# Moving the selection of keys, the products after a scan, and a load within a hybrid decoder layer's kernel

## The chip, the cores and the metric

The kernel runs on one core of a Trainium2 chip. Its time is the device time of one execution in microseconds (us), shown as the median of several runs. The engines are TensorE (PE in the profile; its weight loads are PEld), VectorE (DVE), ScalarE (ACT), GpSimd (POOL) and SyncE (SP), which here only issues transfers. Each engine works through its own queue in order, and engines wait for one another by semaphores.

## The reference, cut to what matters

One layer of a decoder runs for a prompt of 1040 rows (16 learned rows and 1024) and for 64 sample rows. All rows are normed and projected by one wide matrix `w_in`. Branch A keeps for each query the 256 best admissible keys by an index score and attends over them. Branch B is stick-breaking attention:

```python
z = q @ k.T * HEAD_DIM ** -0.5
log_keep = where(strict, log_sigmoid(-z), 0)
after = reverse_cumsum(log_keep) - log_keep
out = exp(where(strict, log_sigmoid(z) + after, -inf)) @ v
```

The kernel computes branch B without logarithms: the weight of a key is sigmoid(z) times the product of sigmoid(-z) over all later keys up to the query. The product is a scan from right to left, and the weights are one elementwise product after it. Gates, a gated convolutional MLP and a last norm follow; the change does not touch them.

## The kernel before, in words

The program is a row of blocks, each with a barrier at its end: norm, index projections, index scores of samples and prompt, the other projections, stick (branch B), sparse (branch A), sample attention, merge, MLP, last norm. Three of its parts are touched.

**Projections** (`projections`, tag `pr`). Five pairs of column blocks, 512 columns each; the last pair is followed by none. For each half s of pair k PE multiplies nine row tiles (`NT`) by a weight block that is split in a high and a low part (ScalarE L324, VectorE L352, from the raw weights in `w_raw`), and the result goes by a ring of six tiles to the array `proj` in memory (SP L310). VectorE has time over there: it runs a bisection (`Bisection`) for the 256th largest score of every row, over the seven tiles with more than 256 keys (`INDEX_TILES`, widths 384 to 1024 and 1040, 5264 columns together). One bit takes a count per tile (L827) and some small steps; seven bits go into each of five pairs, 35 passes for 31 bits. `part` deals them out over the 18 half-tiles of a pair. The split of the next weights stands behind the fourth tile of a half (`SPLIT_AT`), so VectorE waits there for ScalarE and for nothing else of the matmuls in the last three pairs.

**Selection** turns the threshold into additive masks in bf16 (0 or -1e30): `next_threshold`, seven counts above it, and five steps per tile (`choose`: equality L944, a scan that ranks equals L946, a comparison L948, an addition L950, a scaling L952), 42 parts in all. VectorE takes two parts at the end of each of the first 21 iterations of stick.

**Stick** (`stick`). Four pairs of heads (`PAIRS`), nine query tiles each, so 36 iterations n, with lags written out by hand. Rows of q and k are loaded at the block's start and for each next pair (L1043, L1044), turned by PE (L1091) and copied by ScalarE. For tile t the keys are (t + 1) * 128 columns, 1040 in the last tile, which has only 16 rows. Iteration n:

```python
score(n); turn_qk(...)       # PE L1103, L1109, L1091
turn(n - 3); use(n - 4)      # PE L1122, then L1137
open_tile(n); take_qk(...)   # ScalarE L1178, L1179
take_turns(n - 3)            # ScalarE L1189
scan both heads of n         # VectorE L1219
evacuate(n - 5)              # VectorE L1211
product for both heads of n  # GpSimd L1077
```

`score` makes the scores of a tile in four banks of PSUM, up to 512 columns each; `open_tile` takes two sigmoids from each bank (`rest`, `prob`); VectorE scans `rest`; GpSimd multiplies `prob` by it; `turn` transposes the weights, four tiles to a bank and two banks in turn, which `take_turns` copies; `use` multiplies them by the values into one of two tiles `o`, and waits until the tile two before has been evacuated. Four buffers of `prob` and `rest` let the engines be some tiles apart. The text calls `turn` the turns, `use` the value products and the tile t the tile's number within its pair.

The store of the sample rows' mask stands near the end of SP's queue. The masks have a tensor of their own, which sparse reads.

Of the kernel before, what the change touches and what calls it, by code (L numbers as in the profile page):

```python
# [40 lines left out]
P = 128  # L41
D = 1024
KC = D // P
# [28 lines left out]
NEG = -1e30  # L72
LEAST = -3e38
# [163 lines left out]
def projections(nc, ctx, tag, w_in, cos, sin, hi, lo, w_raw, raw_in, done, proj, head, plain_pairs, behind, search):  # L237
# [52 lines left out]
    with nc.Block() as block:  # L290
        @block.sync
        def _(sp):
# [51 lines left out]
        def _(dve):  # L344
            dve.wait_ge(tables_in, 32)
            turns = Count(turned_by)

# [36 lines left out]
            def body(k, two, following):  # L384
                for s in range(2):
                    for t in range(NT):
# [4 lines left out]
                        if search:  # L391
                            search.part(dve, k, NT * s + t, 2 * NT)
# [274 lines left out]
MASK_AT, MASKS_W = packed(range(NT))  # L667
# [126 lines left out]
class Bisection:  # L794
# [5 lines left out]
    PER = -(-BITS // TURNS)  # L800
# [21 lines left out]
    def count_tile(self, dve, j, op, flags=None):  # L822

        if flags is None:
            t = INDEX_TILES[j]
            flags = self.flags[:, SCORE_AT[t]:SCORE_AT[t] + key_width(t)]
        return dve.tensor_scalar(flags, self.of_tile(j), self.thr[:, j:j + 1], None, op, ALU.add,  # L827
                                 accum_out=self.count[:, j:j + 1])
# [18 lines left out]
    def part(self, dve, i, n, parts):  # L847

        steps, tiles = self.steps, len(INDEX_TILES)
        for x in range(n * self.PER * tiles // parts, (n + 1) * self.PER * tiles // parts):  # L850
# [23 lines left out]
class Selection:  # L874
# [4 lines left out]
    STEPS = 6  # L879
    PER = 5  # L880
    ALL_MADE = 4 + PER * len(INDEX_TILES)

    def __init__(self, nc, ctx, search, masks):
        def sb(name, shape, dt=F32):
            return ctx.enter_context(nc.sbuf_tensor(f"tk_{name}", shape, dt))
        self.search, self.masks = search, masks
        self.equal = [sb(f"equal{b}", [P, NP_ROWS]) for b in range(2)]
        self.rank = [sb(f"rank{b}", [P, NP_ROWS]) for b in range(2)]
        self.low_half, self.high_half, self.carry = (sb(n, [P, len(INDEX_TILES)], I32)
                                                     for n in ("low_half", "high_half", "carry"))  # L890
# [16 lines left out]
    def next_threshold(self, dve):  # L907
# [3 lines left out]
        halves = self.halves  # L911
        dve.tensor_scalar(low_half, mag, 0xFFFF, None, ALU.bitwise_and)
# [14 lines left out]
    def count_above(self, dve, j):  # L927
# [26 lines left out]
    def part(self, dve, n):  # L954

        tiles = len(INDEX_TILES)
        if n == 0:
            self.next_threshold(dve)
# [1669 lines left out]
```

## Time and profile before

| what | value |
|---|---|
| runs shown | 2531.18, 2535.61, 2536.31 us; median 2535.61 |
| profiled execution, its own time | 2532.94 us |
| its span, first to last instruction | 2531.3 us |
| PE, DVE, ACT, POOL busy | 2197.9, 1479.0, 772.8, 182.8 us |
| mean granted clock of PE | 0.941 |

The span is shorter than the execution's time by what lies around it. A busy time is the union of an engine's instructions; PE's matmuls overlap, and their ends are modelled. Shares of the whole span are averages over stages with different limits. The page's chain that ended last holds only the last norm, about 6 us, so the stages have to be read one by one.

### The profile page before, as it was taken

How to read it: one execution, taken by the hardware profiler on the slowest of the kernel's cores; microseconds unless marked ns; L12 is line 12 of the kernel's file. 1: busy time of each engine (PE TensorE's matmuls, PEld its weight loads, DVE VectorE, ACT ScalarE, POOL GpSimd, SP SyncE). 2: the span in 40 equal slices, each digit the busy share in tenths (PEclk: the TensorE clock that was granted, in tenths of full speed). 3: DMA queues.
4: the chain of work that ended last, by engine and by line, in shares of the span. 5: the costliest groups of instructions: out<-in, count | busy, mean ns of one | idle time of the engine just before them, and what ended most of it. 6: DMA issues, size and time to landing. Idle time of an engine off the chain costs nothing. (4 is left out here: it accounts for less than half of the span.)

```text
span 2531.3 us, 37719 instructions
## 1 busy us (share of the span) xinstructions
PE 2197.9 (87%) x13473; PEld 1812.3 (72%) x13473; DVE 1479.0 (58%) x2563; ACT 772.8 (31%) x1449; POOL 182.8 (7%) x141
## 2 busy tenths in 40 slices
PE   3867799999997777788488698979999999999995
PEld 3823488888885555555355487869999999999994
DVE  4416878567574997457144355335655665665566
ACT  4025310121113656567133333122212212221212
POOL 0001000000002677000100000000000000000000
PEclk8978899999998988899699899989999999999998
DMA  3212122222312110220699844011011101111102
GB/s 130 78 37 53 57 84 91 105 83 81 114 50 73 37 37 12 56 73 18 185 367 362 322 147 178 2 46 51 25 50 50 46 29 50 50 33 42 50 17 87
DMA packets 186022, 218.75 MB, mean 86 GB/s; under 512 B 28796, under 2 KB 119292, under 8 KB 184764
## 3 DMA queue, kind: packets, MB, share of 16 engines
q1 hardware_dynamic: 177588, 214.02, 25.7%
q10 hardware_dynamic: 8072, 3.05, 0.5%
q8 instruction: 66, 1.08, 0.2%
q0 software_dynamic: 256, 0.27, 0.1%
q14 instruction: 40, 0.33, 0.0%
HBM read 181.17 MB, written 36.13 MB: 86 GB/s over the span
## 5 line engine op out<-in xcount | busy, mean ns | idle before, releaser
L2385 DVE TENSOR_TENSOR x_all<-x_all,ff_down 128x512 f32<-128x512 f32 x396 | 272.3, 688 | 163.6 <-PE ff_down L2289 158.9
L2274 PE MATMUL ff_up<-m_hi,ff_up_hi 128*128 128x368 f32 x1056 | 348.6, 330 | 7.5 <-DVE ff_up_lo L2362 7.5
L2275 PE MATMUL ff_up<-m_lo,ff_up_hi 128*128 128x368 f32 x1056 | 348.9, 330 | 0.0
L2276 PE MATMUL ff_up<-m_hi,ff_up_lo 128*128 128x368 f32 x1056 | 348.4, 330 | 0.0
L411 PE MATMUL pr_acc<-pr_w_hi,h_hi 128*128 128x512 f32 x720 | 281.5, 391 | 16.2 <-DVE pr_w_lo L352 16.2
L412 PE MATMUL pr_acc<-pr_w_lo,h_hi 128*128 128x512 f32 x720 | 281.3, 391 | 0.0
L413 PE MATMUL pr_acc<-pr_w_hi,h_lo 128*128 128x512 f32 x720 | 281.0, 390 | 0.0
L827 DVE TENSOR_SCALAR_CACHE_REDUCE bi_flags<-scores,bi_thr 128x384 bf16<-128x384 f32 (+6 forms) x252 | 235.4, 993 | 1.3
L2274 PEld LDWEIGHTS ff_up<-m_hi,ff_up_hi 128*128 128x128 f32 x1056 | 199.0, 188 | 8.8 <-DVE ff_up_lo L2362 7.9
L2275 PEld LDWEIGHTS ff_up<-m_lo,ff_up_hi 128*128 128x128 f32 x1056 | 199.0, 188 | 0.9
L2276 PEld LDWEIGHTS ff_up<-m_hi,ff_up_lo 128*128 128x128 f32 x1056 | 198.9, 188 | 0.0
L411 PEld LDWEIGHTS pr_acc<-pr_w_hi,h_hi 128*128 128x128 f32 x720 | 135.8, 189 | 44.8 <-DVE pr_w_lo L352 16.3
L336 ACT ACTIVATE pr_staged<-pr_acc 128x512 f32<-128x512 f32 x72 | 43.1, 599 | 399.8 <-PE pr_acc L413 399.8
L2287 PE MATMUL ff_down<-ff_down_hi,ff_g_hi 128*128 128x512 f32 x396 | 157.5, 398 | 5.8 <-issue 5.8
L1077 POOL TENSOR_TENSOR st_prob<-st_prob,st_rest 128x127 f32<-128x127 f32 (+8 forms) x72 | 155.6, 2184 | 82.4 <-DVE st_rest L1219 82.4
L1219 DVE TENSOR_TENSOR_SCAN st_rest<-st_rest 128x128 f32<-128x128 f32 (+8 forms) x72 | 121.7, 1728 | 65.1 <-ACT st_prob L1179 65.0
L2289 PE MATMUL ff_down<-ff_down_hi,ff_g_lo 128*128 128x512 f32 x396 | 157.1, 397 | 0.0
L2288 PE MATMUL ff_down<-ff_down_lo,ff_g_hi 128*128 128x512 f32 x396 | 157.0, 397 | 0.0
L413 PEld LDWEIGHTS pr_acc<-pr_w_hi,h_lo 128*128 128x128 f32 x720 | 135.9, 189 | 28.3
L412 PEld LDWEIGHTS pr_acc<-pr_w_lo,h_hi 128*128 128x128 f32 x720 | 135.9, 189 | 28.2
L2316 ACT ACTIVATE ff_g_hi<-ff_g 128x1152 fp32r<-128x1152 f32 x22 | 25.7, 1168 | 299.9 <-DVE ff_g L2370 299.9
L352 DVE TENSOR_TENSOR pr_w_lo<-w_raw,pr_w_hi 128x2048 fp32r<-128x2048 f32 x20 | 44.9, 2288 | 118.1 <-ACT pr_w_hi L324 118.1
(283 smaller groups left out, 3728.3 us busy)
## 6 DMA issues: line engine op xcount, KB each, us to landing
out_proj<-pr_staged SPq DMA_DIRECT2D x90, 256.0 KB, 2.0
up_raw<-in_w_up SPq DMA_DIRECT2D x44, 512.0 KB, 5.0
w_raw<-in_w_in SPq DMA_DIRECT2D x10, 2048.0 KB, 7.9
sa_keys<-in_cache_k_a SPq DMA_DIRECT2D x64, 256.0 KB, 4.3
sa_keys<-in_cache_k_b SPq DMA_DIRECT2D x64, 256.0 KB, 7.3
sa_values<-in_cache_v_a SPq DMA_DIRECT2D x64, 256.0 KB, 7.8
sa_values<-in_cache_v_b SPq DMA_DIRECT2D x64, 256.0 KB, 5.4
ff_down_raw<-in_w_down SPq DMA_DIRECT2D x22, 512.0 KB, 3.6
```

The source lines that it names most:

```text
L411: pe.matmul(out, hi[:, c, at], w_hi[s][:, c, 0:width], start=c == 0, stop=False)
L412: pe.matmul(out, hi[:, c, at], w_lo[s][:, c, 0:width], start=False, stop=False)
L413: ins = pe.matmul(out, lo[:, c, at], w_hi[s][:, c, 0:width], start=False, stop=c == KC - 1)
L827: return dve.tensor_scalar(flags, self.of_tile(j), self.thr[:, j:j + 1], None, op, ALU.add, accum_out=self.count[:, j:j + 1])
L1077: pool.tensor_tensor(x, x, rest[g % R][hh][0:r, 1:w], ALU.mult).then_inc(weighed, 1)
L2274: pe.matmul(up[n][:], w, hi[:, c, at], start=c == 0, stop=False)
L2275: pe.matmul(up[n][:], w, lo[:, c, at], start=False, stop=False)
L2276: ins = pe.matmul(up[n][:], w_rest, hi[:, c, at], start=False, stop=c == KC - 1)
L2287: pe.matmul(down[n][:], g_hi[:, at], down_hi[:, cols], start=True, stop=False)
L2288: pe.matmul(down[n][:], g_hi[:, at], down_lo[:, cols], start=False, stop=False)
L2289: pe.matmul(down[n][:], g_lo[:, at], down_hi[:, cols], start=False, stop=True).then_inc(down_done, 1)
L2385: dve.tensor_tensor(at, at, down[n][:], ALU.add).then_inc(down_added.sem, 1)
```

## The change

1. The bisection has 28 bits in the first four pairs and its last 3 in the first half of the last pair. The selection runs in the second half of that pair, on VectorE, 42 parts over nine tiles. Its steps are recast: a [P,1] step, an equality that gives 2^100 or 0 in bf16, a scan, a comparison with a product, and one step that makes the mask.
2. The masks lie over the scores of their own tile; the two full tiles' masks lie behind them. The selection's scratch tiles lie in `w_raw`, behind the rows below. `w_raw` lives until sparse has ended.
3. The first pair's rows of q and k for stick are loaded into `w_raw` during the last half block of the projections, after the last weight split and after all stores of the pairs before.
4. In stick, the products after the scan move from GpSimd to VectorE, behind both scans of the tile. The value products of tile n - 4 stand ahead of the turns of tile n - 3. Results of tiles 0 to 3, 4 to 7 and 8 of a head pair share a bank, and are evacuated by one copy each. The store of the sample mask moves to the head of SP's queue.

The diff, cut to its core (signatures and renamed arguments are left out):

```diff
@@ projections, SyncE @@
                     if coming:
                         sp.wait_ge(lo_made, 2 * k + s + 1)
                         load(coming)
+                    elif load_ahead:
+                        sp.wait_ge(lo_made, 2 * k + s + 1)
+                        for b in range(RING):
+                            sp.wait_ge(stored[b], 16 * 3 * k)
+                        load_ahead(sp)
...
@@ projections, VectorE @@
-                        if search:
-                            search.part(dve, k, NT * s + t, 2 * NT)
+                        if selection and following:
+                            search.part(dve, k, NT * s + t, 2 * NT, search.PER)
+                        elif selection and s == 0:
+                            search.part(dve, k, t, NT, search.LAST)
+                        elif selection:
+                            selection.part(dve, t, NT)
...
-MASK_AT, MASKS_W = packed(range(NT))
+MASK_AT = {t: 2 * SCORE_AT[t] for t in INDEX_TILES}
+MASK_AT.update({t: 2 * SCORE_AT[NT - 1] + key_width(NT - 1) + at for t, at in packed(range(FULL_T))[0].items()})
...
@@ Bisection @@
-    PER = -(-BITS // TURNS)
+    PER = 7
+    LAST = BITS - PER * (TURNS - 1)
...
@@ Selection @@
-    ALL_MADE = 4 + PER * len(INDEX_TILES)
+    PARTS = len(INDEX_TILES) * (1 + PER)
+    ALL_MADE = 3 + PER * len(INDEX_TILES)
...
+        self.search = search
+        self.masks = search.scores[:].bitcast(BF16)
+        self.rank = spare[:, 0:NP_ROWS]
+        self.equal = spare[:, NP_ROWS:NP_ROWS + NP_ROWS // 2].bitcast(BF16)
...
-    def count_above(self, dve, j):
-
-        ins = self.search.count_tile(dve, j, ALU.is_gt, self.of_tile(INDEX_TILES[j]))
+    def count_not_above(self, dve, j):
+
+        ins = self.search.count_tile(dve, j, ALU.is_le)
...
         if step == 0:
-            dve.tensor_scalar(eq, self.search.of_tile(j), self.search.thr[:, j:j + 1], None, ALU.is_equal).then_inc(ended, 1)
+            dve.tensor_scalar(need, search.count[:, j:j + 1], BIG, BIG * (TOPK - w), ALU.mult, ALU.add).then_inc(ended, 1)
         elif step == 1:
+            dve.tensor_scalar(eq, search.of_tile(j), search.thr[:, j:j + 1], BIG, ALU.is_equal, ALU.mult).then_inc(ended, 1)
+        elif step == 2:
             dve.tensor_tensor_scan(rk, eq, eq, 0.0, ALU.add, ALU.bypass).then_inc(ended, 1)
-        elif step == 2:
-            dve.scalar_tensor_tensor(rk, rk, self.search.need[:, j:j + 1], eq, ALU.is_le, ALU.mult).then_inc(ended, 1)
         elif step == 3:
-            dve.tensor_tensor(eq, rk, self.of_tile(t), ALU.add).then_inc(ended, 1)
+            dve.scalar_tensor_tensor(rk, rk, need, eq, ALU.is_le, ALU.mult).then_inc(ended, 1)
         else:
-            dve.tensor_scalar(self.of_tile(t), eq, -1.0, -NEG, ALU.add, ALU.mult).then_inc(ended, 1)
...
+            dve.scalar_tensor_tensor(self.of_tile(t), search.flags_of(j), -BIG, rk, ALU.mult, ALU.add).then_inc(ended, 1)
...
+        for x in range(n * self.PARTS // parts, (n + 1) * self.PARTS // parts):
+            if x == 0:
+                self.next_threshold(dve)
+            if x < tiles:
+                self.count_not_above(dve, x)
+            else:
+                self.choose(dve, *divmod(x - tiles, self.PER))
...
@@ stick @@
+    O_GROUPS = [(0, 4), (4, 8), (8, NT)]
+    group_of = [next(k for k, (a, b) in enumerate(O_GROUPS) if a <= t < b) for t in range(NT)]
...
-    o = [ctx.enter_context(nc.psum_tensor(f"st_o{b}", [P, P], F32)) for b in range(2)]
+    o = [ctx.enter_context(nc.psum_tensor(f"st_o{b}", [P, 4 * P], F32)) for b in range(2)]
...
@@ stick, SyncE @@
-            load_qk(0)
+            selection.store(sp, sample_mask, mask_stored)
...
-            selection.store(sp, sample_mask, mask_stored)
-            sp.wait_ge(o_out, NG)
+            sp.wait_ge(mask_stored, 16)
+            sp.wait_ge(o_out, PAIRS * len(O_GROUPS))
...
@@ stick, GpSimd @@
             selection.allow_all(pool)
-            for g in range(NG):
-                r, w = tile_rows(g % NT), key_width(g % NT)
-                for hh in range(2):
-                    pool.wait_ge(scanned, 2 * g + hh + 1)
-                    x = prob[g % R][hh][0:r, 0:w - 1]
-                    pool.tensor_tensor(x, x, rest[g % R][hh][0:r, 1:w], ALU.mult).then_inc(weighed, 1)
...
@@ stick, TensorE: use(g) @@
-                if g >= 2:
-                    pe.wait_ge(o_out, g - 1)
+                b = i * len(O_GROUPS) + group_of[t]
+                first, last = O_GROUPS[group_of[t]]
+                at = (t - first) * P
+                if t == first and b >= 2:
+                    pe.wait_ge(o_out, b - 1)
...
-                        ins = pe.matmul(o[g % 2][half(hh), 0:r], v_rows[i % 2][0:w, kt, half(hh)],
-                                        prob_t[g % 2][hh][0:w, kt, 0:r], start=kt == 0, stop=kt == t)
+                        ins = pe.matmul(o[b % 2][half(hh), at:at + r], v_rows[i % 2][0:w, kt, half(hh)],
+                                        prob_t[g % 2][hh][0:w, kt, 0:r], start=kt == 0, stop=kt == t,
+                                        skip_group_check=True)
...
+                if n >= USE_LAG:
+                    use(n - USE_LAG)
                 if TURN_LAG <= n < NG + TURN_LAG:
                     turn(n - TURN_LAG)
-                if n >= USE_LAG:
-                    use(n - USE_LAG)
...
@@ stick, VectorE @@
+            def evacuate(i, k):
+                first, last = O_GROUPS[k]
+                b = i * len(O_GROUPS) + k
+                dve.wait_ge(used, i * NT + last)
+                if k == 0 and i >= 2:
+                    dve.wait_ge(stored[i % 2], 16 * (i // 2))
...
+                w = min(last * P, NP_ROWS) - first * P
+                dve.tensor_copy(o_all[i % 2][:, first * P:first * P + w], o[b % 2][:, 0:w]).then_inc(o_out, 1)
...
+                for hh in range(2) if n < NG else ():
+                    dve.wait_ge(scanned, 2 * n + hh + 1)
+                    x = prob[n % R][hh][0:r, 0:w - 1]
+                    dve.tensor_tensor(x, x, rest[n % R][hh][0:r, 1:w], ALU.mult).then_inc(weighed, 1)
                 if n >= USE_LAG + 1:
-                    evacuate(n - USE_LAG - 1)
-                selection.part(dve, 2 * n)
-                selection.part(dve, 2 * n + 1)
+                    i, t = divmod(n - USE_LAG - 1, NT)
+                    if t + 1 == O_GROUPS[group_of[t]][1]:
+                        evacuate(i, group_of[t])
...
@@ program @@
+                w_raw = index_scope.enter_context(nc.sbuf_tensor("w_raw", [P, KC, 512], F32))
+                behind_weights = w_raw[:].rearrange("p c n -> p (c n)")
+                q_rows, k_rows = (behind_weights[:, ROWS * k:ROWS * (k + 1)].rearrange("p (t n) -> p t n", t=NT)
+                                  for k in range(2))
+                selection = Selection(nc, index_scope, search, behind_weights[:, 2 * ROWS:])
...
+                def load_stick(sp):
+                    sp.dma_start(q_rows, tiled[:, :, O_QB:O_QB + P]).then_inc(stick_in, 16)
+                    sp.dma_start(k_rows, tiled[:, :, O_KB:O_KB + P]).then_inc(stick_in, 16)
```

## Rows read from the trace of the kernel before

**Rows 1.** Busy time by stretch, two stages: us, then PE, PEld, DVE, ACT, POOL; clock, DMA
```profile
268.00:780.00 512.00, 493.51 (x2168) 407.70 (x2164) 347.14 (x782) 81.90 (x99) 1.66 (x7) 0.98 0.24 84
780.00:1032.00 252.00, 191.67 (x1536) 135.97 (x1536) 198.00 (x166) 147.45 (x385) 157.02 (x78) 0.86 0.14 38
```

**Rows 2.** The same view, the stick stage by head pair
```profile
791.70:838.20 46.50, 35.08 (x216) 21.63 (x216) 44.00 (x51) 32.49 (x83) 27.61 (x16) 0.84 0.21 53
838.20:901.50 63.30, 48.26 (x386) 35.08 (x385) 58.96 (x46) 36.52 (x96) 39.54 (x19) 0.87 0.17 45
901.50:959.60 58.10, 45.58 (x387) 32.07 (x386) 53.21 (x38) 36.27 (x96) 44.13 (x18) 0.91 0.07 20
959.60:1030.00 70.40, 58.65 (x536) 43.48 (x534) 41.82 (x34) 39.40 (x104) 44.29 (x21) 0.85 0.03 11
```

**Rows 3.** Timeline of PE, six score products, one group of value products: start us, us, operation
```profile
808.52 2.01 PE L1103 MATMUL st_banks<-st_k_t,st_q_t 64*128 64x512 f32 x8
...
923.99 2.08 PE L1103 MATMUL st_banks<-st_k_t,st_q_t 64*128 64x512 f32 x4
...
928.12 1.35 PE L1103 MATMUL st_banks<-st_k_t,st_q_t 64*128 64x512 f32 x8
...
935.53 1.77 PE L1103 MATMUL st_banks<-st_k_t,st_q_t 64*128 64x512 f32 x8
...
959.59 0.72 PE L1103 MATMUL st_banks<-st_k_t,st_q_t 64*128 64x128 f32 x4
...
963.16 1.53 PE L1137 MATMUL st_o<-st_prob_t,st_v_rows 128*64 128x128 f32 x24
...
978.63 2.08 PE L1103 MATMUL st_banks<-st_k_t,st_q_t 64*128 64x512 f32 x4
```

**Rows 4.** Who waited for whom, 923.99 to 978.63: us in total, times, longest
```profile
PE st_turned L1122 <- ACT st_prob_t L1189: 3.6, 4, 1.2
...
PE st_turned L1122 <- POOL st_prob L1077: 2.3, 1, 2.3
...
PE st_o L1137 <- DVE st_o_all L1211: 0.6, 1, 0.6
```

**Rows 5.** Timeline of POOL, stick stage, two of its product groups
```profile
805.51 2.97 POOL L1077 TENSOR_TENSOR st_prob<-st_prob,st_rest 128x511 f32<-128x511 f32 x2 [1.99 <-DVE st_rest L1219]
...
933.43 33.43 POOL L1077 TENSOR_TENSOR st_prob<-st_prob,st_rest 128x639 f32<-128x639 f32 x12 [1.43 <-DVE st_rest L1219]
```

**Rows 6.** Timeline, last pair: two pairs of scans, one group of value products
```profile
975.01 3.68 PE L1137 MATMUL st_o<-st_prob_t,st_v_rows 128*64 128x128 f32 x32
...
982.36 2.34 DVE L1219 TENSOR_TENSOR_SCAN st_rest<-st_rest 128x512 f32<-128x512 f32 x2 [7.58 <-ACT st_prob L1179]
...
1001.36 7.32 DVE L1219 TENSOR_TENSOR_SCAN st_rest<-st_rest 128x1024 f32<-128x1024 f32 x2
```

**Rows 7.** Groups by line, whole span: busy us, mean ns; idle before
```profile
L1801 DVE COPY sa_keys_t<-sa_turned 128x512 f32<-128x512 f32 x64 | 44.2, 690 | 60.6 <-PE sa_turned L1586 48.8 <-DMA sa_masks<-sample_mask 11.7
...
L2369 DVE TENSOR_TENSOR ff_g<-ff_g,ff_b_sb 128x1040 f32<-128x1040 f32 x22 | 27.2, 1238 | 7.6 <-ACT ff_b_sb L2331 7.6
...
L946 DVE TENSOR_TENSOR_SCAN tk_rank<-tk_equal 128x384 f32<-128x384 f32 (+6 forms) x7 | 18.0, 2577 | 0.1
...
L950 DVE TENSOR_TENSOR tk_equal<-tk_rank,masks 128x384 f32<-128x384 f32 (+6 forms) x7 | 13.8, 1965 | 0.1
...
L1837 DVE TENSOR_TENSOR_SCAN sa_least<-sa_soft 128x1032 f32<-128x1032 f32 x4 | 9.2, 2298 | 0.0
...
L2370 DVE TENSOR_TENSOR ff_g<-ff_g,ff_b_sb 128x64 f32<-128x64 f32 x22 | 4.8, 219 | 0.0
```

**Rows 8.** Timeline, first product of the stick stage
```profile
787.00 1.11 PE L1091 MATMUL st_banks<-c_ident,st_q_rows 128*128 128x128 f32 x4 [9.26 <-DMA st_k_rows<-out_proj]
```

**Rows 9.** Timeline of DVE, last projection block: its weight split, its last search step
```profile
705.85 4.50 DVE L352 TENSOR_TENSOR pr_w_lo<-w_raw,pr_w_hi 128x2048 fp32r<-128x2048 f32 x2 [16.82 <-ACT pr_w_hi L324]
...
754.09 0.16 DVE L871 TENSOR_SCALAR bi_bit<-bi_bit 128x7 int32<-128x7 int32 x1
```

More of the change, by code:

```diff
@@ L72 @@
 NEG = -1e30
+BIG = 2.0 ** 100
 LEAST = -3e38
@@ L234, with projections @@
 PLAIN0, PLAIN_PAIRS = O_KB, 3
-def projections(nc, ctx, tag, w_in, cos, sin, hi, lo, w_raw, raw_in, done, proj, head, plain_pairs, behind, search):
+def projections(nc, ctx, tag, w_in, cos, sin, hi, lo, w_raw, raw_in, done, proj, head, plain_pairs, behind, selection, load_ahead):
     def sb(name, shape, dt=F32):
@@ L346, in _ @@
             turns = Count(turned_by)
+            search = selection.search if selection else None
             def split(k, s, block):
@@ L845, in begin, with part @@
         dve.wait_ge(self.begun, 4)
-    def part(self, dve, i, n, parts):
+    def part(self, dve, i, n, parts, bits):
         steps, tiles = self.steps, len(INDEX_TILES)
-        for x in range(n * self.PER * tiles // parts, (n + 1) * self.PER * tiles // parts):
+        for x in range(n * bits * tiles // parts, (n + 1) * bits * tiles // parts):
             b, j = divmod(x, tiles)
@@ L874, with __init__ @@
 class Selection:
-    STEPS = 6
     PER = 5
-    ALL_MADE = 4 + PER * len(INDEX_TILES)
[L883 to L890, printed above, removed]
+    PARTS = len(INDEX_TILES) * (1 + PER)
+    ALL_MADE = 3 + PER * len(INDEX_TILES)
+    def __init__(self, nc, ctx, search, spare):
+        self.search = search
+        self.masks = search.scores[:].bitcast(BF16)
+        self.rank = spare[:, 0:NP_ROWS]
+        self.equal = spare[:, NP_ROWS:NP_ROWS + NP_ROWS // 2].bitcast(BF16)
+        self.low_half, self.high_half, self.carry = (
+            ctx.enter_context(nc.sbuf_tensor(f"tk_{n}", [P, len(INDEX_TILES)], I32))
+            for n in ("low_half", "high_half", "carry"))
         self.halves, self.ended, self.causal = (nc.alloc_semaphore(f"tk_{n}") for n in ("halves", "ended", "causal"))
@@ L911, in next_threshold @@
         halves = self.halves
+        dve.wait_ge(search.steps.sem, search.steps.at(search.TURNS - 1, search.STEPS * search.LAST - 1))
         dve.tensor_scalar(low_half, mag, 0xFFFF, None, ALU.bitwise_and)
@@ L981, in load_exp_ln, with stick @@
                                                  act_func_set_id=EXP_LN_SET))
-def stick(nc, ctx, proj, ident, selection, sample_mask, out_t):
+def stick(nc, ctx, proj, ident, q_rows, k_rows, qk_in, selection, sample_mask, out_t):
     def sb(name, shape, dt=F32):
@@ L2521, in program @@
                         projections(nc, ctx, "pr", a["w_in"], a["cos"], a["sin"], hi, lo, w_raw, raw_in, 2, proj,
-                                    HEAD_PAIRS, PLAIN_PAIRS, None, search)
-                masks = index_scope.enter_context(nc.sbuf_tensor("masks", [P, MASKS_W], BF16))
+                                    HEAD_PAIRS, PLAIN_PAIRS, None, selection, load_stick)
                 with ExitStack() as ctx:
-                    stick(nc, ctx, proj, c["ident"], Selection(nc, ctx, search, masks), sample_mask, out_ts[1])
+                    stick(nc, ctx, proj, c["ident"], q_rows, k_rows, stick_in, selection, sample_mask, out_ts[1])
                 with ExitStack() as ctx:
-                    sparse(nc, ctx, proj, c["ident"], masks, out_ts[0])
+                    sparse(nc, ctx, proj, c["ident"], selection.masks, out_ts[0])
         with nc.cleanup_on_exit():
```

54 lines of the change are left out of this document (17 added, 37 removed).

## The prediction, made before the changed kernel was run

> **What bounds the kernel now.** I read the stages first. The projections hold TensorE (PE) busy for 494 of 512 us [rows 1]: nothing done beside them there is worth time unless it outlasts PE. The stick stage behind them (780 to 1032) has no such engine: of 252 us PE is busy 192, VectorE 198, GpSimd 157, ScalarE 147, at a granted clock of 0.86 [rows 1]. The reader should see four engines that wait for one another.
>
> The split by head pair [rows 2] separates two causes. A pair lasts 46.5, 63.3 and 58.1 us, the last with its drain 70.4; VectorE is busy 93% of the first three while the selection's steps are mixed in. They end in iteration 20, so the cycle from the fourth score of pair 2 to that of pair 3 is free of them: 923.99 to 978.63, **54.64 us** [rows 3]. In that cycle PE waits 3.6 us for ScalarE's copies of turned tiles, 2.3 for GpSimd and 0.6 for VectorE [rows 4]. Behind these is a slowdown by company. GpSimd ran 12 products from 933.43 for 33.43 us without a gap, though one of 511 columns takes 2.97 / 2 = 1.49 us, 2.9 ns a column [rows 5]; its twelve (columns 639, 767, 895, 1023, 1039, 127, each twice, 8,980 in all) would take 26. Beside them two scans of 1024 columns took 7.32 us [rows 6]; a scan of 1032 with GpSimd idle takes 2.298 [rows 7], so a pair 4.6.
>
> The Trainium skill (SBUF — State Buffer, Who interferes with whom) says that a VectorE instruction with two SBUF inputs and a GpSimd instruction that reads SBUF share a port, and that the later one blocks fully. The direction agrees with the rows, the degree does not: 26 us of products and some 19 of scans fitted into 33.4. By the rule alone the pair would be the two added up, some 58 us now, and VectorE's own sum afterwards, which is the first rival's case; the sum below goes by the rows.
>
> **Part 1: search ends earlier, selection moves into the last projection block.** Beside 777.74, where PE's last projection product ends (787.00 less 9.26) [rows 8], VectorE's work has to fit. After the last weight split (710.35) it did 41 of the block's 49 counts until 754.25 [rows 9], 1.07 us each with its share of small steps. Now 14 counts are left there: until 725.3. Then comes the selection. Per tile: a [P,1] step (0.2), a scan (mean width 752, so 752/1032 x 2.298 = 1.68), two two-input steps (0.94 each by the prices of part 3, 1.0 with the gap) and an equality, taken as dear as these [rows 7]: 4.9 us, with 7 tiles 34; seven counts 7; the next threshold 1.7. Together 43, ending near **768**, 10 us ahead of PE. Cost: nothing, covered by PE's products; if the cover fails, the overrun is paid in full at the block's end. The bf16 equality tile is a form that the trace lacks; it is priced as its float32 form, and a stretch of 1.54, as the stick stage's scan shows (2,577 ns [rows 7] against 1,675), is the upper bound: 66 us, 14 too late. The four counts dropped from the 35 passes cost nothing either way.
>
> **Part 2: rows loaded there.** SP gets one wait on the split and six on stores of earlier blocks, all met before its first store of the last nine; two issues pass the stores of that block, no store is held. PE then need not wait from 781 to 787.00 for the row DMAs [rows 8]: **5.8 us** gained, between 0 (if another thing holds PE at the block's start, a rival) and 6. The sample mask's store moves to the front of SP's queue, 0.5 us ahead of the first value rows, which are needed only four iterations later: nothing.
>
> **Part 3: products on VectorE.** A pair has 11,296 scan columns and 11,278 product columns. Scans: 11,296 x 2.298/1032 = 25.2 us. Products: 1,238 ns for 1040 columns and 219 for 64 give 1.044 ns a column and 152 ns each [rows 7]: 11.8 + 18 x 0.152 = 14.5. Three evacuations instead of nine: 2 x 0.69 + 0.15 = 1.5 [rows 7]. VectorE's sum: **41.2 us** a pair, below the cycle of 54.64.
>
> **Part 4: value products ahead of turns.** PE's value products of tile n-4 now fill the time in which ScalarE opens tile n, and its turns come when ScalarE is nearly free for their copies. Of the 3.6 us that PE waits for these copies [rows 4] I take 3.0 as gone; the six short chunks of the narrow tile still alternate. The waits for GpSimd (2.3) and per-tile evacuation (0.6) go. Value products that follow a wait run slower: 32 in 3.68 us at 975.01 [rows 6]; 24 took 1.53 at 963.16 [rows 3], so 2.0 were due. I take these 1.7 back and, as an estimate, 1.1 of the like in the narrow tile's iteration.
>
> **Part 5: a new wait.** The first value product of a pair needs the previous pair's tiles 4 to 7 evacuated, which VectorE does after scans and products of tile 3, one iteration ahead of PE. From the score of tile 3 (978.63) its scans start 3.73 later and take 2.34 [rows 3, 6]; two products of 511 (1.37) and the copy (0.7) bring 8.2 us. PE gets there about 5.9 after the same score (4.1 to the next one, 928.12 less 923.99 [rows 3], and some 1.8 for that). PE waits **2.3 us** a pair, its turns and scores queued behind. Between 0 (VectorE early) and 4. The Trainium skill (Perfetto Trace Analysis, Matmuls) wants independent groups in rotating banks, so that one's evacuation overlaps the next's products; four tiles in one bank give up a part of that. Without the wait the sum would be 7 us better.
>
> **The sum.** The cycle: 54.6 - 3.0 - 2.3 - 0.6 - 2.8 + 2.3 = **48 us** a pair; call it L. Start: 5.8. First pair: the score of tile 6 came 16.8 us after the first (808.52 [rows 3]) before the selection held anything; tiles 6 to 8 take 24.1 in the cycle (935.53 to 959.59 [rows 3]); less GpSimd's 2.3 and some 2 for the moved value products I take 20. So 36.8 for 46.5: 9.7. Pairs 1 and 2: 63.3 + 58.1 - 2L = 25.4. Last pair: its drain beyond a cycle is 70.4 - 54.6 = 15.8, of which I let 1.2 go with GpSimd: 70.4 - (L + 14.6) = 7.8. Gain 48.7 us, in general 192.7 - 3L. The profiled execution took 2532.94 us (span 2531.3, 1.6 around it); it stands 2.7 below the median shown, within the spread of the runs. 2532.9 - 48.7 = **2484 us**.
>
> **The rivals.** *VectorE alone sets the pace.* If three iterations of slack hide PE's waits and the new one, L falls to 41.2: gain 69.1, 2464. For it: VectorE's tiles 4 to 8 alone cost 30 us a pair. Against: over tiles 0 to 3 PE and ScalarE have more to do than VectorE. 0.17. *PE and ScalarE stay as slow as now.* If their alternation and the lower clock eat what the order saves, L is 53: gain 33.7, 2499. For it: granted clock 0.91 even in the third pair [rows 2]. 0.18. *The selection outlasts the projections* by up to 14 us: 2498. Against: GpSimd, in whose company these steps were slow, is busy 1.7 us in that stage [rows 1]. 0.05. *The early rows bring nothing*, since barrier, masks or the table of ScalarE hold PE at the start anyway: 2490. 0.05. *Slower:* the two-input products on VectorE are slow by themselves, not by company. Place: VectorE's queue in every iteration. If products cost 2.6 ns a column (1,965 ns for 752, what the selection's two-input add, L950, took in the stick stage [rows 7]) and scans 2.83, half-way from 2.23 to L946's 2,577/752 = 3.43 [rows 7], VectorE has 18 x 0.15 + 29.3 + 32.0 + 1.5 = 65.5 a pair: with some of the new wait L = 66, a loss of 5, 2538. It decides from L = 64.2. Against: 1,238 ns for 1040 with GpSimd idle [rows 7]. 0.03.
>
> **How the numbers follow.** Forecast 0.52, rivals 0.17, 0.18, 0.05, 0.05, 0.03. The range runs from VectorE's floor (2464) to L = 54.6, the present cycle with only the start and the selection's room gained (2504); it leaves out the slower case, the part of the first rival that ends below its floor, and little else: under 2 in 10. 0.2% (5 us) is about what a measurement of this kernel can tell from no change: faster 0.95, same 0.02, slower 0.03.
>
> **What would show it.** Right: no VectorE work of the selection after 780, the last mask near 768; first product of the stick stage near 781; VectorE's scans of 1024 at 2.3 us and products of 1023 at 1.2; scores of the same tile 48 us apart; PE waiting for the evacuation once a pair. Wrong: scans still above 3 us with GpSimd idle; a pair above 54; a VectorE end later than 778; or a wait on PE for GpSimd's mask at the start.

## The result, and the profile after

The changed kernel took **2491.69 us** (median of four runs, 2489.80 to 2495.26) beside 2535.39 for the kernel before (the three runs shown above and a fourth, 2535.16): ratio 0.9837, 95% interval 0.9822 to 0.9853. Forecast were 2484 and a range of 2464 to 2504. The profiled execution took 2491.59 us, 41.4 less than the one of before, with a mean granted clock of 0.947 for 0.941.

Busy time by stretch, then by head pair (columns as in [rows 1, 2]):

```profile
268.00:780.00 512.00, 492.85 (x2162) 407.53 (x2160) 356.06 (x763) 81.23 (x98) 1.66 (x7) 0.98 0.24 87
780.00:990.00 210.00, 182.07 (x1536) 125.80 (x1536) 156.41 (x156) 148.74 (x385) 1.43 (x6) 0.91 0.14 40
...
783.42:819.69 36.27, 31.32 (x217) 19.54 (x217) 34.50 (x34) 31.83 (x82) 0.00 (x0) 0.95 0.32 85
819.69:871.13 51.44, 46.14 (x386) 32.04 (x385) 39.35 (x40) 36.84 (x97) 0.00 (x0) 0.90 0.17 47
871.13:922.73 51.60, 46.20 (x385) 31.94 (x384) 39.14 (x40) 36.83 (x97) 0.00 (x0) 0.90 0.09 27
922.73:988.07 65.34, 56.24 (x535) 40.30 (x534) 43.41 (x45) 40.75 (x106) 0.00 (x0) 0.91 0.02 9
```

The projections take as long as before, with 9 us more of VectorE in them. The stick stage's last store moved from 1029.86 to 988.07, 41.8 us: 8.3 by the earlier first score, 10.2 in the first pair (46.5 to 36.3), 18.4 in the next two (63.3 and 58.1 to 51.4 and 51.6), 4.9 in the last. What lies behind the stage took as long as before (1501.4 and 1501.8 us).

The timeline of PE, at the start (answering to [rows 8]) and around the narrow tile (to [rows 3, 6]):

```profile
780.25 2.16 PE L1094 MATMUL st_banks<-c_ident,w_raw 128*128 128x128 f32 x18 [3.18 <-PEq L291]
783.42 0.49 PE L1106 MATMUL st_banks<-st_k_t,st_q_t 64*128 64x128 f32 x4 [1.01 <-ACT st_k_t L1175]
...
918.05 2.02 PE L1143 MATMUL st_o<-st_prob_t,st_v_rows 128*64 128x128 f32 x20
920.00 1.54 PE L1125 MATMUL st_turned<-c_ident,st_prob 128*128 128x128 f32 x6
...
934.62 1.97 PE L1143 MATMUL st_o<-st_prob_t,st_v_rows 128*64 128x128 f32 x32
936.52 0.67 PE L1125 MATMUL st_turned<-c_ident,st_prob 16*128 16x16 f32 x8
...
938.48 1.63 PE L1106 MATMUL st_banks<-st_k_t,st_q_t 64*128 64x512 f32 x4
940.03 1.22 PE L1112 MATMUL st_banks<-st_forbidden,c_ident 128*128 128x128 f32 x4
941.19 2.22 PE L1143 MATMUL st_o<-st_prob_t,st_v_rows 128*64 128x16 f32 x36
943.34 0.69 PE L1125 MATMUL st_turned<-c_ident,st_prob 128*128 128x128 f32 x2
943.96 2.51 PE L1106 MATMUL st_banks<-st_k_t,st_q_t 64*128 64x512 f32 x8
...
947.55 0.70 PE L1143 MATMUL st_o<-st_prob_t,st_v_rows 128*64 128x128 f32 x4
```

The 32 value products that took 3.68 us now take 1.97. But the eight scores of the next-but-one tile, 1.35 before, take 2.51: in this execution the slow stretch moved from ahead of the narrow tile's work to behind it, and lasts longer.

Who waited, in the cycle from the fourth score of a pair to that of the next, 886.88 to 938.48 (answering to [rows 4]: total, times, longest):

```profile
DVE st_rest L1227 <- ACT st_prob L1186: 12.5, 5, 4.0
...
PE st_turned L1125 <- ACT st_prob_t L1196: 2.7, 5, 1.1
...
PEld st_turned L1125 <- DVE st_prob L1232: 2.0, 2, 1.4
...
PE st_banks L1106 <- ACT st_prob L1186: 1.3, 1, 1.3
PE st_banks L1094 <- ACT st_prob L1186: 1.2, 4, 0.4
```

VectorE sits idle for 12.5 of 51.6 us because ScalarE has not opened the next tile. PE is busy for 46.2 us and waits 5.2, all of it for ScalarE (2.7, 1.3 and 1.2): these two set the pair. Nobody waits for the evacuation in this cycle; another execution of the same kernel does (f0_after_again). VectorE's timeline at the block's end, and its groups in the stick stage (busy us, mean ns):

```profile
705.18 4.49 DVE L359 TENSOR_TENSOR pr_w_lo<-w_raw,pr_w_hi 128x2048 fp32r<-128x2048 f32 x2 [17.87 <-ACT pr_w_hi L330]
...
763.46 1.24 DVE L964 SCALAR_TENSOR_TENSOR scores<-bi_flags,w_raw 128x1040 bf16<-128x1040 bf16 x1
785.11 0.76 DVE L1227 TENSOR_TENSOR_SCAN st_rest<-st_rest 128x128 f32<-128x128 f32 x2 [20.41 <-ACT st_prob L1186]
...
945.51 0.68 DVE L1219 COPY st_o_all<-st_o 128x512 f32<-128x512 f32 x1
...
L1227 DVE TENSOR_TENSOR_SCAN st_rest<-st_rest 128x1024 f32<-128x1024 f32 x8 | 17.9, 2274 | 0.0
...
L1232 DVE TENSOR_TENSOR st_prob<-st_prob,st_rest 128x1023 f32<-128x1023 f32 x8 | 9.3, 1208 | 0.0
```

### The profile page after: what moved, and what is told of

It reads as the page before. It is cut to its first block and busy times, and to the rows that moved or that the text cites. A ratio compares the mean times of both kernels' runs of the same rounds, so it can differ in the third digit from the quotient of the medians.

```text
span 2489.9 us, 37593 instructions
## 1 busy us (share of the span) xinstructions
PE 2184.9 (88%) x13473; PEld 1799.0 (72%) x13473; DVE 1446.7 (58%) x2534; ACT 774.3 (31%) x1449; POOL 27.3 (1%) x69
## 5 line engine op out<-in xcount | busy, mean ns | idle before, releaser
L841 DVE TENSOR_SCALAR_CACHE_REDUCE bi_flags<-scores,bi_thr 128x384 bf16<-128x384 f32 (+6 forms) x231 | 215.9, 992 | 1.2
L1227 DVE TENSOR_TENSOR_SCAN st_rest<-st_rest 128x128 f32<-128x128 f32 (+8 forms) x72 | 101.4, 1448 | 57.8 <-ACT st_prob L1186 57.6
L1598 PE MATMUL sa_turned<-c_ident,sa_keys 128*128 128x128 f32 x512 | 77.4, 291 | 33.8 <-DVE sa_keys_t L1813 23.6
```

What stands on the lines that cost most here:

```text
L841: return dve.tensor_scalar(self.flags_of(j), self.of_tile(j), self.thr[:, j:j + 1], None, op, ALU.add, accum_out=self.count[:, j:j + 1])
L1227: dve.tensor_tensor_scan(x[:, ::-1], x[:, ::-1], x[:, ::-1], 1.0, ALU.mult, ALU.bypass).then_inc(scanned, 1)
```

## The experiments

Eleven runs were made, in three groups, each group beside the kernel before on one chip. Ratios are to the kernel before, with 95% intervals, and they are what to compare across groups; the pairs are the distances of their first scores in the profiled execution, the last one up to its store; the wait is PE's for ScalarE's copies of turned tiles over the whole stick stage. The profile is of one execution each. What lies behind the stage, which no edit touches, took 1497.6 to 1505.2 us in them, and the stage itself 204.7 and 199.6 us in two executions of the changed kernel, so a difference of a few us between two profiles can be chance.

| kernel | median us | ratio | pairs, us | wait, us |
|---|---|---|---|---|
| before | (own control) | 1 | 46.5, 63.3, 58.1, 70.3 | 19.7 |
| after | 2491.69 | 0.9837 [0.9822, 0.9853] | 36.3, 51.4, 51.6, 65.3 | 11.8 |
| e1_pool | 2489.76 | 0.9835 [0.9815, 0.9855] | 36.3, 51.5, 51.9, 62.5 | 11.8 |
| e2_order | 2500.80 | 0.9876 [0.9861, 0.9891] | 39.1, 52.6, 55.6, 63.7 | 23.1 |
| e3_both | 2496.39 | 0.9867 [0.9851, 0.9884] | 39.9, 51.4, 52.7, 64.0 | 22.0 |
| e4_rows | 2502.30 | 0.9878 [0.9857, 0.9899] | 37.0, 50.4, 50.2, 65.7 | 11.4 |
| e5_parts12 | 2501.73 | 0.9877 [0.9856, 0.9898] | 40.7, 55.2, 53.9, 68.1 | 13.9 |
| e6_stick | 2515.48 | 0.9930 [0.9911, 0.9949] | 40.3, 58.8, 59.6, 64.5 | 11.4 |
| f1_chunks | 2490.74 | 0.9831 [0.9813, 0.9850] | 35.1, 50.0, 51.3, 65.7 | 12.5 |
| f4_mask16 | 2484.19 | 0.9807 [0.9790, 0.9824] | 36.8, 48.4, 48.4, 63.0 | 12.6 |
| f0_after_again | 2487.31 | 0.9834 [0.9820, 0.9847] | 35.1, 50.2, 52.0, 62.3 | 11.5 |
| f5_mask16_chunks | 2486.52 | 0.9824 [0.9811, 0.9838] | 37.9, 49.8, 49.3, 64.2 | 13.7 |
| f6_qk_early | 2483.82 | 0.9815 [0.9801, 0.9828] | 38.0, 46.9, 49.8, 64.0 | 15.6 |

**e1_pool: products back on GpSimd.**

```diff
-                for hh in range(2) if n < NG else ():
-                    dve.wait_ge(scanned, 2 * n + hh + 1)
...
-                    dve.tensor_tensor(x, x, rest[n % R][hh][0:r, 1:w], ALU.mult).then_inc(weighed, 1)
+            for g in range(NG):
...
+                    pool.tensor_tensor(x, x, rest[g % R][hh][0:r, 1:w], ALU.mult).then_inc(weighed, 1)
```

> The changed kernel with one part undone: GpSimd does the products of the stick stage again, VectorE the scans alone. Theory C (the products' company on GpSimd beside VectorE's scans lengthened both and held the pair): the time from the first score of one steady pair to that of the next goes from 51.6 us back to 55 or more, scans of 1024 columns go from 2274 ns to about 2950, and the kernel takes 2491.7 + 2 x 3 to 4 + 3 = about 2502 to 2506 us. Theory Q (the order on TensorE's queue shortened the pair, whoever does the products): the pair stays within 1 us of 51.6 and the kernel at 2489 to 2495, though the scans are long again. Theory A (TensorE and ScalarE alternate and set the pair; VectorE has 12 us of slack in it): as Q, unless the scan and the product of one tile in a row, 2.95 + 3 us instead of 2.27 + 1.2, come too late for the turn of that tile; then 53 to 55 per pair.

Its third pair, and the groups of VectorE and GpSimd:

```profile
871.51:923.36 51.85, 46.36 (x385) 32.01 (x384) 39.77 (x23) 36.85 (x97) 41.08 (x19) 0.90 0.09 27
...
L1086 POOL TENSOR_TENSOR st_prob<-st_prob,st_rest 128x1023 f32<-128x1023 f32 x8 | 31.8, 3993 | 0.0
L1233 DVE TENSOR_TENSOR_SCAN st_rest<-st_rest 128x1024 f32<-128x1024 f32 x8 | 30.0, 3788 | 0.0
```

The company is back and stronger than expected: a scan of 1024 columns takes 3788 ns for 2274 (the 2950 expected is near the mean of the kernel before, which mixes scans of 2.2 and of 3.7 us; see the last section). Yet the pair is the same within 0.3 us, at the same granted clock of 0.90, and the kernel's ratio is the same too. Theory C falls: with the selection gone and the order changed, scans and products have room enough, and who does the products costs nothing that can be measured. Q and A both fit this run. The Trainium skill (SBUF — State Buffer, Who interferes with whom) has these two block each other fully. In turn they would take 2.27 us and, by an estimate from [rows 5] (2.9 ns a column), 2.97 for a product: 5.2 per head. Measured is one of each in 3.8 to 4.0, so the direction holds and the degree does not.

**e2_order: turns ahead of value products again.**

```diff
-                if n >= USE_LAG:
-                    use(n - USE_LAG)
                 if TURN_LAG <= n < NG + TURN_LAG:
                     turn(n - TURN_LAG)
+                if n >= USE_LAG:
+                    use(n - USE_LAG)
```

> The changed kernel with one part undone: on TensorE's queue a tile's turn stands ahead of the value products of an earlier tile again; the products stay on VectorE. Theory Q: the waits of TensorE for ScalarE's copies come back and a steady pair takes 55 us or more instead of 51.6, the kernel 2501 to 2506 us. Theory C: within 3 us of 2491.7, as the products on VectorE brought the shorter pair and the order only spares the ends of TensorE's waits. Both parts adding up halfway: about 2497.

PE's waits in the stick stage, of this kernel and of the changed one:

```profile
PE st_turned L1125 <- ACT st_prob_t L1196: 23.1, 20, 3.2
```
```profile
PE st_turned L1125 <- ACT st_prob_t L1196: 11.8, 20, 2.0
```

Theory Q holds: 9.1 us lost by the medians (0.0039 by the ratios, whose intervals do not overlap), and the waits for the copies double. The median falls just short of the 2501 to 2506 expected, and one of the two steady pairs short of 55 us (52.6 and 55.6). 11.3 us of wait over four pairs is 2.8 a pair. Whom PE waits for ahead of its turns depends on the kernel, the sum does not: copies and GpSimd together are 22.0 us in the kernel before (19.7 and 2.3), 23.1 here, 23.0 in e3_both and 21.9 in e5_parts12, but the copies' 11.8 and no more in the changed kernel and in e1_pool, and 11.4 to 15.6 of the copies in the others with the new order.

**e3_both: both undone.**

> Both undone at once: products on GpSimd and turns ahead of value products, so that of the change only the earlier end of the selection, the mask over the scores and the earlier load of the rows are left. If the start of the stage (8 us) and the first pair, no longer beside the selection (10 us), are what these bring, the kernel takes 2535.4 - 18 to 19, and some more for the second pair, which had the selection's masks beside it before (63.3 to 58.1, 5 us): 2510 to 2517 us, with steady pairs of 58 us. If C and Q add up, e1 and e2 together lose as much as e3. If either part alone had been enough, e1 and e2 lose nearly nothing and e3 loses all of some 20 us.

2496.4, lower than the 2510 to 2517 expected, and 4.4 below e2_order, where only one of the two is undone (the intervals of the two ratios overlap). So the two don't add up, and the steady pair without them is about 52 rather than 58 us. It ran at granted clocks of 0.96 and 0.94, so the 51.6 us of the changed kernel at 0.90 are no like measure; e4_rows, with the new order, has 50.4 and 50.2 at 0.97. Whether something beside the two had been holding the pairs of the kernel before is asked by e5_parts12.

**e4_rows: rows loaded at the stage's start.**

```diff
+            load_qk(0)
             selection.store(sp, sample_mask, mask_stored)
```

> The changed kernel with the rows of the first head pair loaded at the start of the stick stage as before, not in the last projection block. If the wait for these rows alone makes the later start: the first turn waits for the DMA again, the first score moves from 783.4 to about 791 us, and the kernel takes 6 to 8 us more, 2498 to 2500. If TensorE's start is held by something else there (the mask, the last projection copies, or the clock), 2490 to 2494.

```profile
790.54 4.10 PE L1095 MATMUL st_banks<-c_ident,w_raw 128*128 128x128 f32 x18 [9.37 <-DMA w_raw<-out_proj]
```

10.6 us more (0.0041 by the ratios), above the 6 to 8 expected. In the profiled execution 4.1 of them are not the rows: the projections' last product began at 780.79 for 776.68, a difference that other executions show without this edit (the first score comes at 781.6 to 787.5 in those with the early load). From there to the first score it is 14.5 us for 6.7: 7.8 for the rows, 6.2 of it the wait for the DMA (9.37 for 3.18) and most of the rest the turns of the rows behind that wait, 4.10 us for 2.16.

**e5_parts12: parts 1 and 2 of the prediction alone.** As e3_both, and each tile's result evacuated by itself again:

```diff
-    o = [ctx.enter_context(nc.psum_tensor(f"st_o{b}", [P, 4 * P], F32)) for b in range(2)]
+    o = [ctx.enter_context(nc.psum_tensor(f"st_o{b}", [P, P], F32)) for b in range(2)]
...
-                if t == first and b >= 2:
-                    pe.wait_ge(o_out, b - 1)
+                if g >= 2:
+                    pe.wait_ge(o_out, g - 1)
```

> The stick stage of the kernel before as a whole (products on GpSimd, turns ahead of value products, one evacuation per tile into two small tiles); only the selection and the first rows stay where the change put them. Beside e3_both only the evacuation is undone. Theory S (the selection's steps in VectorE's queue were what made the pairs of the kernel before long): as e3_both, 2493 to 2500 us, pairs of 51 to 53 us. Theory G (the evacuation by groups is what shortens the later pairs: in the kernel before, TensorE's value products stood idle 17.6 us in the stage behind copies that VectorE reached late): 2505 to 2515 us, with TensorE waiting for st_o_all 10 us or more again. Theory R of the prediction (54.6 us is the pair without selection): 2510 or more.

Its steady pairs, its wait for the evacuation, and that of e3_both:

```profile
822.37:877.53 55.16, 46.04 (x387) 32.56 (x385) 38.52 (x28) 36.39 (x96) 38.78 (x19) 0.89 0.17 47
877.53:931.43 53.90, 44.44 (x386) 32.17 (x384) 34.79 (x27) 36.27 (x96) 36.62 (x18) 0.92 0.07 22
...
PE st_o L1144 <- DVE st_o_all L1218: 6.4, 5, 2.9
```
```profile
PE st_o L1149 <- DVE st_o_all L1225: 0.7, 3, 0.2
```

2501.7: between theories S and G. The evacuation by groups takes 5.7 us of these waits away, most of it in the last pair (5.2 of the 6.4); what that is worth in time is not shown, since the ratios differ by 0.0010 (2.5 us) with intervals that nearly coincide. The pairs of 55.2 and 53.9 lie around the 54.64 that [rows 3] had shown as the old stage's own pair. They are longer than those of e3_both by 3.7 and 1.2 us, but PE's idle time in them only by 0.4 and 0.5 (9.1 and 9.5 us for 8.7 and 9.0); the rest is PE's busy time, at granted clocks of 0.89 and 0.92 for 0.96 and 0.94. So the 52 us of e3_both are largely the faster PE of that execution, and only in a small part the grouping. The earlier selection and the rows alone bring 0.0123 of the time, 31 us, three quarters of the gain.

**e6_stick: the stick parts alone,** in the kernel before (products, order and groups as in the change; selection and first load where they were).

> The other half alone: the kernel before with products on VectorE, value products ahead of turns and evacuation by groups, while the selection stays in the first 21 iterations of the stick stage and the rows are loaded at its start. If the stick parts have a worth of their own (order 4 to 9 us, as e2_order and e3_both lost), 2523 to 2528 us. If VectorE is then the bound as long as the selection runs (some 83 us of scans and products of two pairs, 5 of three more tiles and the selection's steps, about 45 us without company and 66 as in the kernel before, against 132 us from 791.7 to 924.0 now), its first 21 iterations end at 925 to 946, and what the later ones gain is eaten: 2527 to 2550 us.

```profile
889.16:948.77 59.61, 45.34 (x385) 31.14 (x385) 55.80 (x52) 37.05 (x97) 0.00 (x0) 0.89 0.10 29
...
PE st_o L1136 <- DVE st_o_all L1212: 9.2, 1, 9.2
...
L946 DVE TENSOR_TENSOR_SCAN tk_rank<-tk_equal 128x1024 f32<-128x1024 f32 x1 | 2.3, 2292 | 0.0
```

18 us faster, better than either theory. VectorE is the bound there, 55.8 of 59.6 us, and there company was dear: without GpSimd the selection's seven scans (950, 1226, 1481, 1757, 2012, 2292 and 2314 ns) average 1719 ns for 2577 [rows 7], and its five steps over the seven tiles (L944 to L952) take 33.6 us together for 64.4. But VectorE has the products to do instead, and its busy time of the stage hardly falls (195.5 for 198.0 us); which of the three edits brought the 18 us was not taken apart. The new wait of the prediction's part 5 appears as well, 9.2 us at once in this pair. Alone the two halves bring 31 and 18 us, together 41. The intervals, 0.002 of the time for each half, hardly tell this from a plain sum; that part of what the stick parts save has no one waiting for it where the selection is gone is a likely reading, not a shown one.

**f1_chunks: eight tiles to a chunk of the narrow tile's turns.**

```diff
-    TURNS = [(g, hh, k0, min(4, g % NT + 1 - k0)) for g in range(NG) for hh in range(2) for k0 in range(0, g % NT + 1, 4)]
+    TURNS = [(g, hh, k0, min(8 if g % NT == NT - 1 else 4, g % NT + 1 - k0)) for g in range(NG) for hh in range(2)
+             for k0 in range(0, g % NT + 1, 8 if g % NT == NT - 1 else 4)]
```

> The changed kernel with the turns of the narrow tile (16 rows) in chunks of eight tiles rather than four: 4 copies by ScalarE instead of 6, and 2 fewer changes between TensorE and ScalarE per pair. If this alternation, and the half-speed stretch of TensorE behind it, is the rest of the 3.0 and 2.8 us that the prediction took as gone: 1.5 to 3 us less per pair, 2480 to 2486 us. If the changes are covered by other work of either engine: 2489 to 2494 us.

No gain (2490.7 us), and PE's wait for the copies is as long as before, 12.5 us for 11.8: the short chunks were covered, and were not what was left.

**f4_mask16: the causal mask's products on bf16.**

```diff
-    forbidden = sb("forbidden", [P, P])
+    forbidden = sb("forbidden", [P, P], BF16)
+    one16 = sb("one16", [P, P], BF16)
...
-                    pe.matmul(banks[c % NS][0:r, at], ident[0:r, 0:r], forbidden[0:r, 0:r], start=False, stop=True,
+                    pe.matmul(banks[c % NS][0:r, at], one16[0:r, 0:r], forbidden[0:r, 0:r], start=False, stop=True,
```

> The changed kernel with the causal mask's products in the stick stage on bf16 operands instead of float32 (the mask holds 0 and -1e30, the other operand is the unit matrix, so only the value of the very negative number is rounded). They take 0.71 us per tile for two heads, 6.4 us per pair. If TensorE's queue is what sets the pair of 51.6 us (46.2 busy): 3 to 5 us less per pair, 2473 to 2481 us for the kernel. If ScalarE or the chain through all engines sets it: 2488 to 2494 us. It is also possible that a less busy TensorE is granted the lower clock in longer stretches, which would give a part of it back: 2481 to 2488.

Its third pair and its mask products, then those of the changed kernel:

```profile
867.92:916.35 48.43, 41.79 (x368) 27.35 (x367) 39.12 (x40) 36.83 (x97) 0.00 (x0) 0.93 0.12 35
...
L1114 PE MATMUL st_banks<-st_forbidden,st_one 128*128 128x128 bf16 x64 | 9.7, 236 | 0.0
```
```profile
L1112 PE MATMUL st_banks<-st_forbidden,c_ident 128*128 128x128 f32 x128 | 25.1, 323 | 0.0
```

15.4 us of PE's work are gone, and the steady pairs are 3.0 and 3.2 us shorter than in the changed kernel's first profile (granted clock 0.93 for 0.90), 1.8 us shorter than the shortest in its second, f0_after_again (0.97): PE's queue is a bound of the pair. The median, 2484.2, misses the 2473 to 2481 of that theory alone and lies in the range in which the clock gives a part back. The first pair does not shrink (36.8 for 36.3), and there the granted clock is 0.91 for 0.95.

**f0_after_again, f5_mask16_chunks, f6_qk_early.** The second is f4 and f1 together; the third has this beside:

```diff
-    QK_WITH = {6: (0, 1), 7: (2, 3), 8: (4,)}
+    QK_WITH = {4: (0, 1), 5: (2, 3), 6: (4,)}
```

> The changed kernel itself, unaltered, on the chip that runs the next two, so that these can be compared with it: 2489 to 2495 us.

> The bf16 mask products and the narrow tile's turns in chunks of eight together. If TensorE's queue sets the pair and each change takes its own piece out of it, the sum of both gains, 7.5 + 1 us or a little more as TensorE has less else to wait for: 2481 to 2484 us. If the chunks bring nothing (they were within the spread alone): 2484 as with the mask alone.

> As the run before, and the turns of the next pair's rows two tiles earlier, with tiles 4 to 6 instead of 6 to 8. The spacing of the scores in the changed kernel is 4.3 and 3.5 us after tiles 4 and 5 but 6 to 9 us after tiles 6 to 8, where ScalarE has both its longest sigmoids and the copies of these rows, and TensorE waits for it. If ScalarE binds in these tiles and TensorE elsewhere, an even spread is worth 1 to 3 us per pair: 2474 to 2480. If TensorE binds throughout, or the lag of the queues evens it out already: 2481 to 2485.

The changed kernel, unaltered, by head pair:

```profile
785.02:820.15 35.13, 29.97 (x216) 18.53 (x216) 33.36 (x34) 31.74 (x82) 0.00 (x0) 1.00 0.27 71
820.15:870.37 50.22, 43.16 (x385) 30.00 (x384) 40.58 (x40) 36.96 (x97) 0.00 (x0) 0.97 0.19 54
870.37:922.41 52.04, 46.49 (x386) 32.14 (x385) 39.42 (x40) 36.85 (x97) 0.00 (x0) 0.90 0.09 26
922.41:984.66 62.25, 51.41 (x535) 37.32 (x534) 43.12 (x45) 40.56 (x106) 0.00 (x0) 1.00 0.03 10
```

Its waits for the evacuation, one in the second pair and one in the last, and their sum over the stage:

```profile
842.98 0.44 PE L1143 MATMUL st_o<-st_prob_t,st_v_rows 128*64 128x128 f32 x4 [1.73 <-DVE st_o_all L1219]
945.21 0.44 PE L1143 MATMUL st_o<-st_prob_t,st_v_rows 128*64 128x128 f32 x4 [1.73 <-DVE st_o_all L1219]
...
PE st_turned L1125 <- ACT st_prob_t L1196: 11.5, 19, 2.0
...
PE st_o L1143 <- DVE st_o_all L1219: 3.5, 2, 1.7
```

The first pair of f5_mask16_chunks:

```profile
782.42:820.33 37.91, 31.41 (x199) 17.38 (x199) 35.35 (x34) 31.74 (x82) 0.00 (x0) 0.86 0.33 86
```

The same program has pairs of 50.2 and 52.0 us beside granted clocks of 0.97 and 0.90, and a last pair of 62.3 at 1.00 for 65.3 at 0.91: the stage is 5 us shorter than in the first profile, beside a higher clock in three of its four pairs. The clock is not all gain: at 0.97 PE is busy 3.0 us less than in the 51.4 us pair of the first profile, and waits for ScalarE as long as there, but 1.7 us more for the evacuation, so the pair is only 1.2 us shorter. With the bf16 mask the first pair has fewer products and yet takes longer, 37.9 us, at 0.86. The median of f0_after_again lies 2 us below its expectation and that of f5_mask16_chunks 2.5 above its own; the chunks show no gain, with or without the mask. The early turns (f6_qk_early) bring 2.7 us beside f5_mask16_chunks, within the spread of the runs, and land in the range of the second theory, 2481 to 2485. The three kernels with the bf16 mask lie at 0.9807, 0.9824 and 0.9815, the changed kernel at 0.9837 and 0.9834: the best versions are some 0.2% faster than the changed kernel, and only f4's interval lies nearly clear of it. That they beat it is likely rather than settled.

## Why the prediction was right, and where it was off

**Direction and range** came out as forecast; the profiled execution gained 41.4 us where 48.7 were predicted. By stretch, predicted and measured: start 5.8 and 8.3, first pair 9.7 and 10.2, pairs 1 and 2 25.4 and 18.4, last pair 7.8 and 4.9. So the sum was helped by chance: 3.0 us more than forecast at the front offset some of the 9.9 us that the later pairs fell short.

**Part 1** held: the last mask ended at 764.7 (768 forecast), 12 us before PE's last projection product. e5_parts12 shows that this move and the rows carry most of the gain.

**Part 2**: 6.1 us of wait went (9.26 to 3.18 us), 5.8 predicted. From the projections' end to the first score 7.7 us went, as the 18 turns behind the shorter wait ran faster too, 2.16 us. This the prediction left out, and it is not certain: of ten executions with the early load six have these turns at 2.15 to 2.16 us, four at 3.71 to 3.82.

**Part 3**: the price held, 39.1 us of VectorE a pair for 41.2. What fell is the reading put ahead of it, that "behind these is a slowdown by company" in the free cycle. e1_pool brings the company back, at 3788 ns a scan, and the pair stays. (The two scans in 7.32 us that the prediction quotes are of the pair after that cycle; those within it, at 946.72, took as long.) PE's wait of 2.3 us for GpSimd is gone, as forecast, but not by the move: PE has no such wait in e1_pool's third pair either. The 2.0 us in which weight loads wait for VectorE's products (PEld above) run beside PE's matmuls; in the kernel before the same loads waited 2.3 us for GpSimd.

**Part 4, the step that was off.** The pair was to be 48 us; it is 51.6 in the cycle of the first profile, and 50.2 and 52.0 in f0_after_again. Two terms were too large. Of the wait for ScalarE's copies 3.0 us were taken as gone, and 0.9 went in the cycle (3.6 to 2.7 us). And "I take these 1.7 back and, as an estimate, 1.1 of the like" depends on the execution. In the first profile, at 0.90, PE's busy time in the cycle rose from 45.16 to 46.20 us instead of falling by 2.8: the stretch at the lower clock moved behind the narrow tile's turns. In the second pair of f0_after_again, at 0.97, it fell to 43.16 us, by 2.0, but then the new wait of part 5 appeared. With what was measured there, the sum of the prediction is 54.6 - 0.9 - 2.3 - 0.6 - 2.0 + 1.7 = 50.5 us for the 50.2 measured. At neither clock do the terms give 48. The old cycle was also not quite free of the selection, whose last step on VectorE ended 2.1 us into it, at 926.09; as VectorE then idled for 1.6 us until its next scan, that cost nothing.

**Part 5**: the wait was forecast at 2.3 us a pair. In the cycle of the first profile it did not occur: the copy of 0.68 us began at 945.51 and ended 1.4 us before PE's value product at 947.55. That PE's idle time fell by 4.1 us there, near the 3.6 that the waits of parts 3 to 5 had been given in sum, is luck: a slow PE came too late to wait for the copy, and this made up for the copies' term. In f0_after_again the wait is there in two of three pairs, 1.7 us each, at granted clocks of 0.97 and 1.00, and it is missing in the pair at 0.90. When VectorE is late it grows to 9.2 us (e6_stick). The Trainium skill (Perfetto Trace Analysis, Matmuls), which the prediction named for rotating banks, agrees with these waits. The other side of the grouping, nine evacuation waits made three, was 0.6 us in the cycle, but 5.2 in the last pair alone (e5_parts12).

**The rivals**: VectorE's pace did not bind (12.5 us idle a pair). The measured pair lies between the forecast and the rival in which PE and ScalarE stay slow (53 us). The selection did not outlast the projections, the early rows did bring time (e4_rows), and products on VectorE are not slow by themselves (1208 ns for 1023 columns).

## What to carry to other kernels

Take work off an engine's queue where that engine is the bound, and price company only there: a scan that is 67% longer cost nothing once VectorE had slack. When queues are reordered, count the waits taken away over the whole stage, by what the engine does next and not by whom it waits for, since a wait for one engine can turn into a wait for another. Don't book a recovery of the clock in full: the slow stretch can move, and a faster engine meets the next wait sooner. And undo the parts one by one, and profile the same kernel twice: the wait that one execution lacked stood in the other.

## What was not expected of the hardware

In the first pair, less work on PE came with a lower granted clock: with the mask products on bf16 it was 0.91, 0.86 and 0.87 in three kernels, beside 0.94 to 1.00 in five executions with the float32 mask and the changed order (the changed kernel, e1_pool, e4_rows, f1_chunks and f0_after_again). That the one causes the other is argued from these eight, not shown. The later pairs speak against a rule: there the clock was 0.90 to 0.96 with the bf16 mask and 0.89 to 1.00 without.

A scan of 1024 columns took 2980 ns on average in the kernel before and 3788 in e1_pool, but the first is a mean over two kinds. In the first two pairs of the kernel before the two scans of this width took 4.44 and 4.46 us, in the last two 7.32 [rows 6], 3.66 each, which is close to e1_pool. The second pair's scans, on VectorE, and the products on GpSimd that answer to them:

```profile
892.68 4.46 DVE L1219 TENSOR_TENSOR_SCAN st_rest<-st_rest 128x1024 f32<-128x1024 f32 x2
...
895.03 6.30 POOL L1077 TENSOR_TENSOR st_prob<-st_prob,st_rest 128x1023 f32<-128x1023 f32 x2 [2.76 <-DVE st_rest L1219]
```

Here the second scan ran beside the first product and was not slowed; GpSimd had been idle when the scans began. Where the scans took 3.7 us, GpSimd was already at work without a gap [rows 5], and so it was in e1_pool. That this head start makes the difference is argued, not tried.
